# Hybrid block kernel: the first norm's roots put on a diagonal and multiplied into the turn of x, with small loads, constants and two copies moved

## What is computed

```python
def rms_norm(x, gain):
    xf = x.astype(jnp.float32)
    y = xf * lax.rsqrt(jnp.mean(xf * xf, axis=-1, keepdims=True) + EPS)
    return (y * gain.astype(jnp.float32)).astype(x.dtype)
...
    h = rms_norm(x, norm_mix[l])                 # (1, 256, 1024)
    proj = h @ w_in[l]                           # one projection, columns shared out
    q_a, k_a, v_a, z, xbc, dt_raw, q_x, gate_logits = jnp.split(proj, IN_SPLITS, axis=-1)
...                                              # three branches, gates, w_out
    x = x + moe_ffn(rms_norm(x, norm_ffn[l]), ...)   # all 32 experts' weights are read
```

## Time and profile before

| what | us |
|---|---|
| three runs | 1459.51 median (1458.72 to 1461.27) |
| the profiled execution | 1459.15 |
| its span in the profile | 1457.0 |
| outside the span | 2.15 |
| busy: PE, DVE, ACT, POOL | 1426.1, 592.2, 405.9, 63.5 |
| PE's first instruction | 12.95 |
| first `gemm` | 16.38 |

### The profile page before, as it was taken

The page is one execution under the profiler, slowest core; times in us unless marked ns, Lnnn a source line. Parts: engine busy times, 40 slices in busy tenths (PEclk is TensorE's granted clock), DMA queues, the critical chain, the costliest instruction groups (busy, mean ns, idle before and its releaser), DMA issues.

```text
span 1457.0 us, 18622 instructions
## 1 busy us (share of the span) xinstructions
PE 1426.1 (98%) x7575; PEld 820.1 (56%) x7575; DVE 592.2 (41%) x1149; ACT 405.9 (28%) x601; POOL 63.5 (4%) x50
## 2 busy tenths in 40 slices
PE   6999999999999999999999999999999999999998
PEld 6898888777778873444444444444444444433443
DVE  6779788787778552112121121211112111111111
ACT  5766666556535441010110110001011010101110
POOL 5110000111100000000000000000000000000000
PEclk9999999999999999999999999999999999999999
DMA  7455444654563969999999999999999999999996
GB/s 248 153 186 177 155 138 161 196 160 160 173 244 131 379 261 423 428 428 427 429 428 430 428 429 428 429 429 428 429 428 429 428 429 428 429 428 429 428 427 287
DMA packets 74001, 491.27 MB, mean 337 GB/s; under 512 B 5265, under 2 KB 8977, under 8 KB 49377
## 3 DMA queue, kind: packets, MB, share of 16 engines
q1 hardware_dynamic: 71280, 487.57, 82.8%
q10 hardware_dynamic: 2160, 2.62, 0.6%
q0 software_dynamic: 512, 0.43, 0.2%
HBM read 488.93 MB, written 1.07 MB: 336 GB/s over the span
## 4 chain that ended last, share of the span: by engine, by line
PE 80%; DMA 10%; DVE 6%; ACT 2%; issue 2%; DVEq 0%; ACTq 0%; SPq 0%
PE ps L1929 26%; PE ps L1967 13%; PE ps L1590 7%; PE ps L1857 7%; PE ps L1592 7%; PE ps L1591 7%; DMA regions<-in_w_up 6%; PE ps L1577 4%; PE ps L1909 4%; DMA regions<-in_w_gate 3%; DVE regions L1165 2%; DVE splits L1019 2%; PE ps L1804 1%; ACT splits L706 1%; PE ps L1937 1%
## 5 line engine op out<-in xcount | busy, mean ns | idle before, releaser
L1929 PE MATMUL ps<-regions,sig 128*64 128x512 f32 x2048 | 463.4, 594 | 4.5 <-DMA regions<-in_w_gate 4.2
L1929 PEld LDWEIGHTS ps<-regions,sig 128*64 128x64 f32 x2048 | 141.9, 137 | 277.1 <-issue 259.5
L1967 PE MATMUL ps<-regions,tmp 128*64 128x512 f32 x1024 | 225.1, 592 | 0.0
L1590 PE MATMUL ps<-splits,regions_r 128*128 128x512 f32 x512 | 205.8, 402 | 1.9 <-DVE regions_r L1012 1.7
L1592 PE MATMUL ps<-splits,regions_r 128*128 128x512 f32 x512 | 200.1, 391 | 0.0
L1591 PE MATMUL ps<-splits,regions_r 128*128 128x512 f32 x512 | 199.8, 390 | 0.0
L706 ACT ACTIVATE splits<-halves 128x1024 fp32r<-128x1024 f32 x152 | 159.1, 1056 | 100.2 <-PE ps L1592 83.4
L1019 DVE TENSOR_TENSOR splits<-halves,splits 128x1024 fp32r<-128x1024 f32 x132 | 166.0, 1262 | 46.5 <-ACT splits L706 45.1
L892 ACT ACTIVATE work<-work 128x512 f32<-128x512 f32 x32 | 20.1, 629 | 475.4 <-DVE work L1517 475.4
L1967 PEld LDWEIGHTS ps<-regions,tmp 128*64 128x64 f32 x1024 | 71.8, 137 | 131.9 <-issue 129.5
L1857 PEld LDWEIGHTS ps<-craw,regions 128*128 128x128 f32 x1024 | 119.2, 192 | 25.6 <-issue 25.2
(11 more groups left out here) (299 smaller groups left out, 1186.3 us busy)
## 6 DMA issues: line engine op xcount, KB each, us to landing
regions<-in_w_gate SPq DMA_DIRECT2D x64, 2048.0 KB, 29.7
regions<-in_w_up SPq DMA_DIRECT2D x64, 2048.0 KB, 28.0
regions<-in_w_down SPq DMA_DIRECT2D x64, 2048.0 KB, 30.9
halves<-in_w_in SPq DMA_DIRECT2D x48, 1024.0 KB, 5.2
halves<-in_w_br_b SPq DMA_DIRECT2D x8, 1024.0 KB, 5.1
halves<-in_w_mem_kv SPq DMA_DIRECT2D x8, 1024.0 KB, 5.0
halves<-in_w_br_a SPq DMA_DIRECT2D x4, 1024.0 KB, 7.5
halves<-in_w_br_c SPq DMA_DIRECT2D x4, 1024.0 KB, 7.5
```

The source lines that it names most:

```text
L1590: pe.matmul(out, lhs[0], rhs[0], start=start, stop=False, skip_group_check=True)
L1929: last = pe.matmul(ps[64 * h:64 * h + 64, bank, :], xgT[:, 4 * k + c], eslots[slot][:, c, h * NB:(h + 1) * NB], start=(k == 0 and c == 0), ...
L1967: last = pe.matmul(ps[64 * h:64 * h + 64, D_BANK, :], actT[:, c, 64 * k:64 * k + 64], eslots[slot][:, c, h * NB:(h + 1) * NB], start=False ...
```

## The change

It does these things.

- DVE no longer scales the rows. It multiplies `ident` by the two columns of roots into two diagonal tiles `by_rs` (128 x 128 each). PE makes `hT` as an ordinary float32 product of x's rows with these diagonals in place of a transpose.
- The gain comes as 8 rows of 128 (4 KB instead of 0.5 MB), PE turns it once into columns, and ACT and DVE apply it per column when they split the group, in two instructions of 256 columns where there was one of 512.
- `hT` 2 stands behind `gemm` 0 and `hT` 3 behind `gemm` 1. `split` 1 moves behind `hT` 0.
- POOL makes the `shade` tiles first, then waits until both diagonals are written, and only then issues its 15 small loads. `craw` is cleared behind them.
- The 19 constants leave `wdt` for a step of their own, `wdt_kinds`, behind unit 20.
- `xsT` 0, 2, 4 and 6 (the second block after their `xbc` block) stand in front of that place's `take` instead of behind it.

```diff
     at(1, "wdt")
+    at(first("q", 1), "wdt_kinds")
...
         if i < INNER // P // 4:
-            at(w + 8, "xsT", 2 * i)
+            extra[w + 8].insert(0, ("xsT", 2 * i))
             at(w + 9, "xsT", 2 * i + 1)
...
-    s = [("split", 0), ("split", 1), ("rest", 0), ("hT", 0), ("rest", 1), ("hT", 1), ("hT", 2), ("hT", 3),
-         ("split", 2), ("rest", 2)]
+    s = [("split", 0), ("rest", 0), ("hT", 0), ("split", 1), ("hT", 1), ("rest", 1), ("split", 2), ("rest", 2)]
+    at(0, "hT", 2)
+    at(1, "hT", 3)
...
-            sp.dma_start(gain1, g_mix.partition_broadcast(P)).then_inc(sem("gain_landed"), 16)
+            sp.dma_start(gain1_rows, g_mix.rearrange("(c p) -> c p", p=P)).then_inc(sem("gain_landed"), 16)
...
+            pool.wait_ge(sem("rows_scaled"), TT)
             pool.dma_start(rel_raw, rel_rev).then_inc(sem("rel_landed"), 16)
...
+            dve.wait_ge(sem("gain_turned"), 1)
+            dve.tensor_copy(gain1_sb, ps[:, EXP_BANK, 0:KC]).then_inc(sem("gain_ready"), 1)
             dve.wait_ge(sem("row_squares"), 2)
             rstd(rs_x, ss_x, D)
-            dve.wait_ge(sem("gain_landed"), 16)
             for t in range(TT):
-                dve.scalar_tensor_tensor(out=xn[:, t], in0=x_in[:, t], scalar=rs_x[:, t:t + 1], in1=gain1,
-                                         op0=ALU.mult, op1=ALU.mult).then_inc(sem("rows_scaled"), 1)
+                dve.tensor_scalar(by_rs[:, t], ident[:], rs_x[:, t:t + 1], None, ALU.mult).then_inc(sem("rows_scaled"), 1)
...
+                elif kind == "hT":
+
+                    b = group()
+                    for t in range(TT):
+                        pe.wait_ge(sem("rows_scaled"), t + 1)
+                        for j in range(2):
+                            c = 2 * step[1] + j
+                            last = pe.matmul(ps[:, b, j * T + t * P:j * T + (t + 1) * P], x_in[:, t, c * P:(c + 1) * P],
+                                             by_rs[:, t], start=True, stop=True)
+                    last.then_inc(misc_ready, 1)
```

More of the change, by code:

```diff
@@ L627, in _ @@
             pool.iota(iota_i[:], pattern=[[1, BLK]], base=0, channel_multiplier=0).then_inc(sem("iota"), 1)
-            pool.memset(craw[:], 0.0).then_inc(sem("craw_zero"), 1)
+            ones_pairs = ones.rearrange("p (k b) -> p k b", b=2)
+            for half in range(2):
+                at0 = 64 * (1 - half)
+                pool.affine_select(out=shade[:, 2 * half], in_=ones, compare_op=ALU.is_gt, fill=0.0, base=-2 * at0,
+                                   pattern=[[-1, P]], channel_multiplier=2).then_inc(sem("shades"), 1)
+                pool.affine_select(out=shade[:, 2 * half + 1].rearrange("p (k b) -> p k b", b=2), in_=ones_pairs,
+                                   compare_op=ALU.is_equal, fill=0.0, base=at0, pattern=[[1, P // 2], [0, 2]],
+                                   channel_multiplier=-1).then_inc(sem("shades"), 1)
+            pool.wait_ge(sem("rows_scaled"), TT)
             pool.dma_start(rel_raw, rel_rev).then_inc(sem("rel_landed"), 16)
@@ L646, in _ @@
                            norm_ffn.rearrange("(h p c) -> p h c", h=2, p=P)).then_inc(gain2_landed, 16)
[L647 to L654, removed]
+            pool.memset(craw[:], 0.0).then_inc(sem("craw_zero"), 1)
             for step in SCHED:
@@ L706, in _ @@
                     act.activation(hi, raw, ACT.Copy).then_inc(hi_ready, 1)
-                elif kind in ("yT", "memT"):
-                    pair, gain = (ybT, gssm_sb) if kind == "yT" else (memT, gmem_sb)
-                    if step[1] == 0:
+                elif kind in TURNED:
+                    pair, gain = TURNED[kind]
+                    if step[1] == 0 and kind == "hT":
+                        act.wait_ge(sem("gain_ready"), 1)
+                    elif step[1] == 0:
                         act.wait_ge(sem("small_landed"), 16 * 12)
@@ L717, in _ @@
                                            scale=gain[:, c:c + 1]).then_inc(sem(kind + "_rounded"), 1)
-                elif kind in ("hT", "mergedT"):
+                elif kind == "mergedT":
                     for k in range(MISC_GROUPS[kind]):
@@ L987, in _ @@
                 kind = step[0]
-                if kind in ("yT", "memT"):
-                    pair, gain = (ybT, gssm_sb) if kind == "yT" else (memT, gmem_sb)
+                if kind in TURNED:
+                    pair, gain = TURNED[kind]
                     for k in range(MISC_GROUPS[kind]):
@@ L1004, in _ @@
                                 ins.then_inc(misc_taken, 1)
-                elif kind in ("hT", "mergedT"):
-                    both = hT if kind == "hT" else mergedT
+                elif kind == "mergedT":
+                    both = mergedT
                     for k in range(MISC_GROUPS[kind]):
@@ L1196, in _ @@
                     dve.tensor_tensor(wdt_lo, raw, wdt_hi.bitcast(F32), ALU.subtract).then_inc(sem("wdt_ready"), 1)
-                    of_rest = dtw[:, 0, 0:32]
+                elif kind == "wdt_kinds":
+                    of_rest = root_in[:, 0:32]
                     link(dve.tensor_reduce(of_rest, ident[:].rearrange("p (x h) -> p x h", h=4), AX, ALU.add))
@@ L1601, in _ @@
             pe.wait_ge(sem("masks"), 3)
+            pe.wait_ge(sem("gain_landed"), 16)
+            pe.transpose(ps[:, EXP_BANK, 0:KC], gain1_rows, ident[0:KC, 0:KC]).then_inc(sem("gain_turned"), 1)
             n = 0
@@ L1604, in _ @@
                 kind = step[0]
[L1605 to L1611, removed]
+                if kind == "memT":
+                    pe.wait_ge(sem("mem_landed"), 16)
+                    by_columns(lambda t: mem_sb[:, t], step[1])
+                elif kind == "hT":
[7 more added lines that the diff above has]
+                    last.then_inc(misc_ready, 1)
                 elif kind == "gemm":
```

8 lines of the change are left out of this document (5 added, 3 removed).

## The result

| | median us | runs |
|---|---|---|
| before | 1459.35 (1458.36 to 1461.27) | 20 |
| after | 1461.76 (1460.38 to 1463.65) | 20 |

What follows compares the result with a forecast made beforehand. The stream of expert weights bounds the end, and its start hangs on PE's place in the front; 0.9 us at dt's columns plus 0.5 for the constants gave 1.4 us slower, predicted 1460.8 us, range 1458.0 to 1463.6.

Steps and rivals of the forecast that it cites:

- The sign: Whole kernel: slower than before, by 1.4 us.
- the class: Whole kernel: no change that can be told, within 0.2% or 2.9 us; given 0.75.
- PE starts at 10.60, gemm 0 at 14.5 behind a hole of 0.5: Start of PE: first product 2.38 us earlier at 10.60, PE still for 0.5 us from 14.0, gemm 0 at 14.5.
- A product costs two passes: PE's hT: a float32 product costs two transpose-size passes, 0.22 us at full clock, 0.43 at half.
- 0.5 us to the half clock: Start of gemm 0: its passes run partly at half clock, taken as 0.5 us lost.
- gemm 3 waits 0.5 for the twelfth load: End of first block: small load lands at 24.1, delaying wdt and group 3's low part; gemm 3 starts 0.5 us late.
- The constants cost 0.5, "If DVE's pace covers it, nothing": Constants behind xsT 4: conv 6 to silu 7 come 1.35 us later, PE loses about 0.5 us near 98 us.
- The swap moves no end: xsT 0, 2 and 6 ahead of the take: moves half a microsecond of ACT's work and no end.
- One to one to the end: Front to end of kernel: a microsecond gained or lost in the front is gained or lost at the end.
- Rival 4: PE's hT at the start: a product costs four transposes, total 1464; chance 0.03.
- Rival 2: Start: DVE holds up POOL's issuing, small loads land 3.7 us later, dt's columns 4.6 us late, 1464.6; chance 0.15.

Runs made afterwards that it cites:

- b_kinds20: Kernel before with two parts of the change alone: constants in their own step behind unit 20, the four xsT ahead of the take; median 1460.41 us, ratio 1.0009.
- a_noswap: Changed kernel with only the swap undone, so xsT 0, 2, 4 and 6 stand behind the take again; median 1462.50 us, ratio 1.0025.
- a_kinds15: Changed kernel with the constants of dt behind unit 15 instead of unit 20; median 1462.08 us, ratio 1.0017.
- a_loads: Changed kernel with POOL's small loads issued at once, without the wait for the diagonals; median 1460.99 us, ratio 1.0010.
- b_swap: Kernel before with one edit: xsT 0, 2, 4 and 6 ahead of the take, constants left in place; median 1459.82 us, ratio 1.0006.
- a_k3: Changed kernel with POOL's small loads issued at once, the swap undone and the constants behind unit 3; median 1460.15 us, ratio 1.0008.
- a_k3_warm: a_k3 plus seven products of the identity, read by nobody, in PE's first hole; median 1461.44 us, ratio 1.0015.
- a_k2: As a_k3, but with the constants behind unit 2; median 1459.28 us beside 1459.49 of before, ratio 1.0000.
- a_warm: Changed kernel plus seven products of the identity, read by nobody, in PE's first hole; median 1462.57 us, ratio 1.0026.
- a_k3_warm_h2: a_k3_warm with the products of group 2 moved in front of gemm 0; median 1460.41 us, ratio 1.0009.

## Why the prediction was right, and where it was off

The sign, the class and the range were right: 1461.76 within 1458.0 to 1463.6, and 1.0 us above the 1460.8. The size was too small: the sum had 1.4 us, the medians show 2.4, and PE's offset against before is 3.0 in the traces. dt's columns came at 29.55 and not at 28.9, and the constants with the swap cost 1.35 and not 0.5. That the median lies as near as 1.0 is partly luck. By its steps:

- *PE starts at 10.60, gemm 0 at 14.5 behind a hole of 0.5.* 9.82, 14.10, a hole of 0.50. The whole lead is 0.4 us better than predicted, since the roots were also ready sooner.
- *A product costs two passes.* Right: 16 passes for eight products, 0.213 apart at half clock and 0.11 at full, 0.81 us per group. The factor of four in the Trainium skill, "TensorE: Matmul & The Clock Gate", section Terms, is not what runs here.
- *0.5 us to the half clock.* 0.69 in the changed kernel. It differs from one execution to the next, so it can't be put down to the change: b_kinds20, with the front of before, lost 1.05 here. Of the seven kernels with products and an idle PE ahead of them, two (the changed one and a_noswap) ran passes of `gemm` 0 at 0.21, a_kinds15 a single one, the other four none. The four that filled the hole had none, and most or all of their products at 0.11.
- *gemm 3 waits 0.5 for the twelfth load.* The mechanism was right and shown by a_loads, where the wait is gone. The term was undersized: 1.4. The load flew 7.1 us, 1.2 more than the 5.9 I took, but was issued at 17.58 and not at 18.2, so it landed 0.6 later than forecast. PE was 0.3 us earlier than forecast, so that more of the lateness showed.
- *The constants cost 0.5, "If DVE's pace covers it, nothing".* This is the step that failed. The 1.35 us by which `conv` 6 is later was right (93.04 less 90.09 is 2.95, of which 1.6 were brought along), and the 0.45 at xsT 7 too. But I took the remaining 0.8 us for absorbed. b_kinds20 shows that they come out near 133 us: DVE's rests are as late at 134.94 as at 92.72, to 0.02 us, so nothing on the line of conv, rest, silu and split takes the lateness up, and PE meets it again at a rest.
- *The swap moves no end.* 0.25 us by b_swap.
- *One to one to the end.* True only to about 1 us. From 445 to 1240 us PE's offset stays within 0.2 us in every kernel. Between 1240 and 1280 us it changes once more, by -0.4 (a_loads, a_k3) to +1.0 (a_k3_warm), +0.6 in the changed kernel. By then the chain of waits has gone over from PE to the loads of weights, or does so there: its first such load of over 40 us starts at 1275.01 before, at 1264.12 in a_k3 and at 1221.77 in the changed kernel. The loads set the end, and their place need not differ by what PE's does; how much it differs in each execution isn't explained. So the offset of 3.0 us at 800 us is 3.6 at the end of the changed kernel and 2.4 in the medians, and a_loads, b_swap, a_k3 and a_k2, at +0.5, -0.6, +0.5 and -0.1 at 445 us, all end 0.1 after before. A lead of PE that reached the end is in none of these runs.
- *Rival 4, four transposes to a product, 4.5 us slower.* It did not come, but its own sum is larger: 3.4 us for the first eight products, 8 x 0.22 = 1.8 for the others, on top of the 1.4.
- *Rival 2, POOL held by DVE.* It did not come: the 12 issues took 7.3 us as before (10.26 to 17.58). What came was its mirror, DVE held by POOL.

Not settled: why all four kernels with seven more products waited 3.7 to 3.8 us for `w_br_a`, where the ten others waited 2.6 to 2.8. That it goes with the products is seen, its cause is not.

## What to carry to other kernels

Work moved off the start isn't hidden by a wait that is about as long as the work: what is left over of it can travel down a chain that has no slack and come out later, at another wait. Add up the length beside what the other engines do there, less the wait, and follow the remainder to the next place where the bound engine waits for that chain, not to the first only. And a load that is held back costs its new issue time and a new flight, which is that of the stretch in which it now flies.

## What the runs showed of the hardware

- A DVE instruction that reads two SBUF tensors stands still while POOL runs a two-input rest, even for two columns. TENSOR_TENSORs of 0.16 to 0.17 us took 1.57, 1.86 and 2.34 us, to the end of POOL's rest each time. A TENSOR_SCALAR of 128x128 float32 in SBUF took 2.35 in place of 0.29. TENSOR_REDUCEs beside POOL's rest kept their 0.19 to 0.21, and two TENSOR_TENSORs of 128x256 with one operand in PSUM their 0.76 (changed kernel, 85.89). The Trainium skill, "VectorE: DVE Perf Modes", section "Mode 2×_2P", says that a float32 tensor_scalar fetches one tensor through both read ports; read that way it would wait for POOL's rest like an instruction with two SBUF inputs, and the 2.35 us agree.
- Small loads issued by POOL flew 1.8 us (x_gains, 2 KB, issued at 14.57) and 7.1 us (b_router, 16 KB, issued at 17.58) in one execution. Before, the same two took 4.9 and 5.9.
- Fourteen passes in a hole of 3.2 us before the real work, with no result that anyone reads, brought the full clock (2.4 GHz) to the products in three of four executions; in a_warm the 16 passes behind them took 2.21 us, against 3.78 in the changed kernel. In a_k3_warm_h2 the first five were still slow.
